# Wide operands for keys and values in a two-layer hybrid decoder step on one Trainium2 core

## What is computed

```
h = rmsnorm(x, g_attn)
(q_a, kv_cmp, kv_slc, kv_win, gate_a, q_b, k_b, v_b, r_b, lr_b, merge) = split(h @ w_in)
kv_slc, kv_win = qk_norm_rows(kv_slc, g_k_slc), qk_norm_rows(kv_win, g_k_win)
o_cmp = cmp_attend(q, compress_kv(past + kv_cmp)); o_slc = top-16 blocks; o_win = window of 512
o_a = sigmoid(gate_a) weighted sum of o_cmp, o_slc, o_win
log_a = log_sigmoid(lr_b @ w_gate_up + b_gate) / 16
o_b, S_new = gla_scan(q_b, k_b, v_b, log_a, state_gla)
x = x + (sigmoid(g_ma) * (o_a @ w_pa) + sigmoid(g_mb) * (o_b @ w_pb)) @ w_out
x = x + (gelu(conv3(h2 @ w_u)) * (h2 @ w_g)) @ w_down,  h2 = rmsnorm(x, g_ffn)
```

## Time and profile before

| | |
|---|---|
| median of three runs | 2159.13 us (2158.03 to 2160.08) |
| the profiled execution, its own time | 2148.94 us |
| its span | 2147.2 us, 30516 instructions |
| PE, matmuls | 2107.1 us, 98% of the span, 11911 records |
| DVE, ACT, POOL | 1144.9, 516.2, 675.8 us (53%, 24%, 31%) |
| mean granted TensorE clock | 0.994 of full speed |
| one weight slot | 512.0 KB, 4.8 us from issue to landing (w_in) |

### The profile page before, as it was taken

How to read it: one execution, slowest core, us unless ns; L and a number is a source line. 1 busy time by engine, 2 the same in 40 slices (tenths; PEclk the granted TensorE clock), 3 DMA queues, 4 the chain that set the end, 5 groups by cost and what they waited for, 6 DMA issues and landing times.

```text
span 2147.2 us, 30516 instructions
## 1 busy us (share of the span) xinstructions
PE 2107.1 (98%) x11911; PEld 1687.4 (79%) x11911; DVE 1144.9 (53%) x2384; ACT 516.2 (24%) x1108; POOL 675.8 (31%) x789
## 2 busy tenths in 40 slices
PE   8999989999999999999999999999999999999999
PEld 7787866678888888888887877666788888888887
DVE  5566746755337455453336666567453454555522
ACT  3124124532112222210122232244221222222000
POOL 5240042204223444434331400621232234444332
PEclk9999999999999999999999999999999999999999
DMA  5874631113222222222284736201132222222222
GB/s 155 273 236 181 248 118 40 41 43 101 79 82 79 79 79 89 90 79 74 68 291 120 267 136 273 81 28 32 59 104 82 79 79 79 79 89 91 79 69 75
DMA packets 172305, 237.53 MB, mean 111 GB/s; under 512 B 39551, under 2 KB 151680, under 8 KB 169408
## 3 DMA queue, kind: packets, MB, share of 16 engines
q1 hardware_dynamic: 153320, 133.11, 20.6%
q0 software_dynamic: 18400, 102.36, 12.8%
q10 hardware_dynamic: 444, 0.12, 0.0%
HBM read 222.76 MB, written 21.11 MB: 114 GB/s over the span
## 4 chain that ended last, share of the span: by engine, by line
PE 91%; DVE 2%; ACT 2%; POOL 2%; DMA 2%; issue 1%; SPq 0%; POOLq 0%; DVEq 0%; ACTq 0%
PE PS L1005 52%; PE PS L948 10%; PE PS L1163 6%; PE PS L970 5%; PE PS L996 3%; PE PS L1499 2%; PE PS L1416 2%; PE PS L460 2%; PE PS L1427 2%; DMA arena<-in_cache_kv_slc_dram,idx 2%; ACT arena L1710 1%; POOL arena L835 1%; PE PS L1374 1%; PE PS L1399 1%; PE PS L1548 1%
## 5 line engine op out<-in xcount | busy, mean ns | idle before, releaser
L1005 PE MATMUL PS<-arena,ring 128*128 128x272 f32 x1632 | 401.3, 393 | 0.9 <-DVE xT L2076 0.6
L1005 PEld LDWEIGHTS PS<-arena,ring 128*128 128x128 f32 x1632 | 309.3, 190 | 65.9 <-issue 2.4
L1710 ACT ACTIVATE arena<-PS 128x272 f32<-128x272 f32 (+12 forms) x442 | 176.1, 423 | 739.6 <-PE PS L1005 286.4
L2076 DVE TENSOR_TENSOR arena<-PS,arena 128x272 f32<-128x272 f32 (+4 forms) x298 | 138.7, 476 | 370.8 <-PE PS L1005 279.4
L1005 PE MATMUL PS<-hT,ring 128*128 128x272 f32 x1120 | 282.3, 397 | 5.9 <-DVE arena L2076 4.7
L1005 PEld LDWEIGHTS PS<-hT,ring 128*128 128x128 f32 x1120 | 213.6, 192 | 52.8 <-DVE arena L2076 5.2
L2076 DVE TENSOR_TENSOR xT<-PS,xT 128x272 f32<-128x272 f32 x224 | 99.0, 442 | 252.2 <-PE PS L1005 251.9
L862 POOL TENSOR_TENSOR qT<-ring 128x512 f32<-128x512 f32 (+1 forms) x38 | 48.8, 1284 | 384.7 <-PE PS L1005 255.7
L2082 DVE SCALAR_TENSOR_TENSOR arena<-arena,prm 128x32 f32<-128x32 f32 (+1 forms) x176 | 143.8, 817 | 22.1 <-ACT arena L1710 18.2
L948 PE MATMUL PS<-hT,ring 128*128 128x272 f32 x640 | 150.7, 394 | 2.3 <-DVE small L2373 1.5
L1005 PE MATMUL PS<-arena,kv_kT 128*128 128x272 f32 x616 | 149.7, 392 | 0.0
(11 more groups left out here) (362 smaller groups left out, 2989.7 us busy)
## 6 DMA issues: line engine op xcount, KB each, us to landing
ring<-in_w_up_dram SPq DMA_DIRECT2D x88, 512.0 KB, 4.6
ring<-in_w_in_dram SPq DMA_DIRECT2D x68, 512.0 KB, 4.8
ring<-in_w_down_dram SPq DMA_DIRECT2D x32, 512.0 KB, 4.4
arena<-in_state_kv_win_dram POOLq DMA_DIRECT2D x4, 2048.0 KB, 8.3
ring<-in_w_out_dram SPq DMA_DIRECT2D x16, 512.0 KB, 4.3
out_dram<-in_state_kv_win_dram POOLq DMA_DIRECT2D x2, 4064.0 KB, 39.6
ring<-in_w_down_dram SPq DMA_DIRECT2D x16, 384.0 KB, 3.5
ring<-in_w_in_dram SPq DMA_DIRECT2D x16, 256.0 KB, 4.6
```

Of the source, the lines that this page charges most:

```text
L1005: mm = pe.matmul(PS[:, bank, 0:HALF], weight[:, k, :], rhs(k), start=(start and k == 0), stop=(stop and k == kc - 1), skip_group_check=not ...
L1710: return nc.scalar.activation(out, in_, func, **kw)
L2076: return nc.vector.tensor_tensor(out, a, b_, op)
```

## The change

Four edits, the same in both layers.

1. `kv1` and `kv2` are multiplied together: a view over two ring slots gives moving operands of 2 x 256 = 512 columns (`wide_few` for the sampled rows, `wide_tiles` for the token tiles). The tickets are `kv12b`, `kv12l` (tiles 0 and 1) and `kv12h` (tiles 2 and 3); ACT copies each out in two parts.
2. The linear branch's values are done the same way from `vb0` and `vb1`, one tile per ticket (`vb0` to `vb3`, and `vbf3` for the sampled rows), at earlier places; `qb` and `kb` come behind them, and the ring's order is changed to fit. The second half of `kb` is split over two places by token halves (`kb1l`, `kb1h`).
3. POOL issues the `S0` loads behind its sums of `hT` and of `rb1`.
4. ACT does one more unit of exponentials ahead of each decay step.

```diff
-    steps = ["q0", "q1", "kv1", "kv2", "kv0", "gl", "qb", "kb", "vb0", "vb1", "rb0", "rb1"]
+    steps = ["q0", "q1", "kv1", "kv2", "kv0", "gl", "vb0", "vb1", "qb", "kb", "rb0", "rb1"]
...
-    at = {("s", 0, 5): ("vb00",), ("s", 0, 4): ("vb01",), ("s", 0, 3): ("qb0",), ("s", 0, 2): ("qb1",), ("s", 0, 1): ("kb0",), ("s", 0, 0): ("kb1",),
-          ("b", 0): ("vb0b", "vb0h"), ("b", 1): ("vb1l",), ("b", 2): ("vb1h", "vb1b"), ("s", 1, 0): ("rb00",), ("u", 0): ("rb01",)}
+    at = {("s", 0, 5): ("vb0",), ("s", 0, 4): ("vb1",), ("s", 0, 3): ("vb2",), ("s", 0, 2): ("vbf3", "vb3"), ("s", 0, 1): ("qb0",),
+          ("s", 0, 0): ("qb1",), ("b", 0): ("kb0",), ("b", 1): ("kb1l",), ("b", 2): ("kb1h",), ("s", 1, 0): ("rb00",), ("u", 0): ("rb01",)}
...
-                for b in range(NB):
-                    gp.dma_start(S0[:, b, :, :], ins["state_gla"][one, b].rearrange("o (a c) k v -> (o c k) a v", c=2)).then_inc(*S.inc(gp, "s0_in", 16))
...
                 in_pieces(low[:, :, HALF:NT], high[:, :, HALF:NT], low[:, :, HALF:NT], ALU.subtract, HALF // 2)
                 gp.nop().then_inc(*S.inc(gp, "g_sum"))
+                gp.nop().then_inc(*S.inc(gp, "settled"))
+                for b in range(NB):
+                    gp.dma_start(S0[:, b, :, :], ins["state_gla"][one, b].rearrange("o (a c) k v -> (o c k) a v", c=2)).then_inc(*S.inc(gp, "s0_in", 16))
...
+            def wide_weights(names):
+
+                for name in names:
+                    pe.wait_ge(*w_landed(pe, name))
+                s0, s1 = sorted(wslot(name)[0] for name in names)
+                return ring[:, s0:s1 + 1:s1 - s0, :].rearrange("p j (k n) -> p j k n", n=WCOLS)
...
+            def wide_tiles(ticket, names, tiles, pool="T"):
+
+                w = wide_weights(names)
+                pe.wait_ge(*S.claim(pe, pool, ticket))
+                b = S.banks(pe, ticket)
+                for j, t in enumerate(tiles):
+                    for k in range(KC):
+                        mm = pe.matmul(PS[:, b + j, :].rearrange("p (j n) -> p j n", j=2), hT[:, k, P * t:P * t + P], w[:, :, k, :], start=(k == 0), stop=(k == KC - 1))
...
-                s = wload("kv1")
-                few("kv1b", s, 256)
-                tm("kv1a", s, 0, 256, 256, range(4))
+                wide_few("kv12b", ("kv1", "kv2"))
+                wide_tiles("kv12l", ("kv1", "kv2"), (0, 1))
...
+                wide_tiles("kv12h", ("kv1", "kv2"), (2, 3))
...
+                def wide_key(ticket, t):
+
+                    act.wait_ge(*S.filled(act, ticket))
+                    b = S.banks(act, ticket)
+                    run(kv[:, t:t + 2, 2, :], PS[:, b:b + 2, 0:256], ACT.Copy)
+                    run(kv[:, t:t + 2, 1, :], PS[:, b:b + 2, 256:512], ACT.Copy).then_inc(*S.drain(act, ticket))
...
+                    if j in DECAY_EXP_AT:
+                        exps(done)
+                        done += 1
                     decay_step(DECAY_EXP_AT.get(j))
...
-                for j in (1, 2):
-                    dv.wait_ge(*S.drained(dv, f"kv{j}a"))
+                for j in "lh":
+                    dv.wait_ge(*S.drained(dv, f"kv12{j}"))
```

More of the change, by code:

```diff
@@ L241, in last_ticket @@
     if name[0] in "qkvr" and name[:2] != "kv":
-        return {"q0": "q1", "q1": "q3", "vb0": "vb0h", "vb1": "vb1b"}.get(name, name + "1")
+        return {"q0": "q1", "q1": "q3", "vb0": "vb3", "vb1": "vb3", "kb": "kb1h"}.get(name, name + "1")
     if name[:2] == "kv":
-        return name + "a"
+        return "kv0a" if name == "kv0" else "kv12h"
     if name[:2] in ("pa", "pb"):
@@ L616, in _ @@
                             (dst[:, :, 24:40], w_in[one, :, O_LR:O_LR + 16].rearrange("o (k p) n -> p (o k) n", p=P))])
-                for name, c0 in (("qb", O_QB), ("kb", O_KB), ("vb0", O_VB), ("vb1", O_VB + 256), ("rb0", O_RB), ("rb1", O_RB + 256)):
+                for name, c0 in (("vb0", O_VB), ("vb1", O_VB + 256), ("qb", O_QB), ("kb", O_KB), ("rb0", O_RB), ("rb1", O_RB + 256)):
                     cols_of(name, w_in, c0)
@@ L980, in few, with wide_few @@
                     mm = pe.matmul(PS[q:q + NS, b, 0:n], hT[:, k, SEQ:NT], w[:, k, :], start=(k < 4), stop=(k >= 4))
+                mm.then_inc(*S.fill(pe, ticket))
+            def wide_weights(names):
[3 more added lines that the diff above has]
+                return ring[:, s0:s1 + 1:s1 - s0, :].rearrange("p j (k n) -> p j k n", n=WCOLS)
+            def wide_few(ticket, names):
+                w = wide_weights(names)
+                pe.wait_ge(*S.claim(pe, "T", ticket))
+                b = S.banks(pe, ticket)
+                for k in range(KC):
+                    q = NS * (k % 4)
+                    mm = pe.matmul(PS[q:q + NS, b, :].rearrange("p (j n) -> p j n", j=2), hT[:, k, SEQ:NT], w[:, :, k, :], start=(k < 4), stop=(k >= 4))
+                mm.then_inc(*S.fill(pe, ticket))
+            def wide_tiles(ticket, names, tiles, pool="T"):
+                w = wide_weights(names)
+                pe.wait_ge(*S.claim(pe, pool, ticket))
+                b = S.banks(pe, ticket)
+                for j, t in enumerate(tiles):
+                    for k in range(KC):
+                        mm = pe.matmul(PS[:, b + j, :].rearrange("p (j n) -> p j n", j=2), hT[:, k, P * t:P * t + P], w[:, :, k, :], start=(k == 0), stop=(k == KC - 1))
                 mm.then_inc(*S.fill(pe, ticket))
@@ L1327, in small_values @@
                     b = S.banks(pe, "vbf")
-                    for name in ("vb0b", "vb1b"):
-                        pe.wait_ge(*S.drained(pe, name))
+                    pe.wait_ge(*S.drained(pe, "vbf3"))
                     pe.matmul(PS[0:NS, b, :], fold4[:, :], vbs, start=True, stop=True).then_inc(*S.fill(pe, "vbf"))
@@ L1766, in _ @@
                     query(r)
-                value_key(1)
+                act.wait_ge(*S.filled(act, "kv12b"))
+                b = S.banks(act, "kv12b")
+                run(kvs[:, 2, :], PS[:, b, 0:256], ACT.Copy)
+                run(kvs[:, 1, :], PS[:, b, 256:512], ACT.Copy).then_inc(*S.drain(act, "kv12b"))
+                wide_key("kv12l", 0)
                 for r in range(R):
                     query_root(r)
-                value_key(2)
+                wide_key("kv12h", 2)
                 act.wait_ge(*S.filled(act, "kvf"))
@@ L2321, in side_copy @@
                             dv.wait_ge(*S.at(dv, "x_stored"))
-                            cc = slice(256 * int(name[2]), 256 * int(name[2]) + 256)
-                            if name[3] == "b":
-                                move = copy(vbs[:, cc], PS[:, b, 0:256])
-                            else:
-                                t0, t1 = {"0": (0, 1), "1": (1, 2), "l": (0, 2), "h": (2, 4)}[name[3]]
-                                move = copy(vT[:, t0:t1, cc], PS[:, b, 0:256 * (t1 - t0)].rearrange("p (t n) -> p t n", n=256))
+                            move = copy(vbs if name == "vbf3" else vT[:, int(name[2]), :], PS[:, b, :])
+                        elif name[-1] in "lh":
+                            a = "lh".index(name[-1])
+                            move = copy(kbT[:, int(name[2]), HALF * a:HALF * a + HALF], PS[:, b, 0:HALF])
                         else:
@@ L2643, in decay_step @@
                     if step == "q":
-                        for name in ("qb0", "qb1", "kb0", "kb1"):
+                        for name in ("qb0", "qb1", "kb0", "kb1l", "kb1h"):
                             dv.wait_ge(*S.drained(dv, name))
```

39 lines of the change are left out of this document (21 added, 18 removed).

## The result

| | before | after |
|---|---|---|
| median | 2159.39 us (2158.03 to 2160.08, 4 runs) | 2183.55 us (2181.72 to 2185.88, 4 runs) |
| the profiled execution | 2148.94 us | 2185.88 us |
| mean granted TensorE clock in it | 0.994 | 0.984 |

The changed kernel is slower by 24.2 us, a ratio of 1.0113 with a 95% interval of 1.0096 to 1.0131. The forecast was 2176.8 in a range of 2164 to 2188, slower with 0.88: the sign was right, the size short by 6.7 us.

A forecast was written before the change was run, and what follows sets the result against it. TensorE was taken as the bound, 91% of layer 0's chain of waits. Terms summed to +8.35 us in layer 0 and +9.35 in layer 1, together +17.7, giving a median of 2176.8 in a range of 2164 to 2188.

The forecast's parts named there:

- Linear values moved forward: Compression loop and behind it: two wide side products on the chain, +3.4 us each; third place loses records, -0.65.
- The two buffer waits: Before the first block scores: PE waits 3.4 us for T0, 5.8 for T1, until DVE drains them; +10.6 per layer.
- Rival B: Before the first block scores: DVE drains T0 and T1 in time, so no waits; 2148 us; chance 0.07.
- The slow clock behind them: At the two new waits before block scores: slow restarts of 1.7 us each, +3.4 per layer, between 0 and 5.
- Rival A: At the new waits: clock not lowered, 3.4 and 1.5 us fall away per layer; +7.9, 2167; chance 0.16.
- Gather stretch: Gathers to second block scores: -1.6 and -0.4 us, slow restart +1.5; together -0.5, between -2.7 and +1.
- State loads and exponentials: Units: PE's waits for POOL and DVE and their restarts go; -6.5 and -5.5 us by layer, -4.2 in each.
- Rival C: Units: gains not had, another wait stands behind the one removed; up to +20 us, half of it 2187; chance 0.10.
- Keys and values: Keys and values, each layer: 64 records of 512 columns replace 128 of 256; -0.6 us, between -1.2 and 0.
- the figure that the prediction had set aside: Keys and values: the Trainium skill's 2.5 ns per record removed, 0.16 us saved, against 0.3 to 0.6 by the rows.
- From profile to median: Whole kernel: median 2159.13 is 10.2 us above the profiled 2148.94; the same difference kept for the forecast, 2176.8.
- Two of the signs: New profile: first block scores 26 to 31 us behind the end of oc, second 25 to 28 behind the gathers' start.

The follow-up runs named there:

- e7: The changed kernel with vb3 ahead of vbf3 and DVE's two copies ahead of the block distances and two transposes; 2154.11 us, ratio to before 0.9976.
- e4: The kernel before with only the linear values wide and moved forward, with the ring order and kb split that go with them; 2198.87 us, ratio 1.0184.
- e8: The changed kernel with both buffer waits kept but filled with extra PE products; 2177.41 us, 6.1 less than the changed kernel.
- e1: The kernel before with only the state loads moved behind POOL's sums; 2146.82 us, ratio 0.9937.
- e2: The kernel before with only one more unit of exponentials ahead of each decay step; 2154.57 us, ratio 0.9974.
- e3: The kernel before with only the keys and values kv1 and kv2 multiplied together; 2159.29 us, ratio 1.0002.
- second profile of before: The kernel before, unchanged, profiled a second time; 2155.30 us in one execution, against 2148.94 in its first profile.

## Why the prediction was right, and where it was short

- **Linear values moved forward** (+3.4 +3.4 -0.65): +6.83 over the stretch with the first two, -0.46 for the third. Right.
- **The two buffer waits** (3.4 and 5.8): 3.74 and 5.82, in both layers, ended by the DVE instructions that were named. Rival B asked for drains by 1.9 and 14 us; they did not come. e7 shows that the waits and their restarts were the whole of it: with other buffers the place costs 1.4 us, and the kernel is 5.2 faster than before, where B had 2148.
- **The slow clock behind them** (1.7 each, 0 to 5 for both) is the term that was mis-sized. It cost 2.9 and 3.0 in either layer (9.98 and 10.05 for 7.13; 10.56 and 10.59 for 7.60), so 2.4 to 2.5 more per layer, 4.9 in all, and above the prediction's own bound of 5 for both in one layer. The first wait was 0.3 longer than forecast too. The step that failed is taking one price from rows of another work: the rows at the units gave 1.6 to 2.6, and the same wait of 3.74 was followed by anything from nothing (e4) to 2.9. Rival A (no clock cost) is out: e8 takes the cost away by keeping PE busy.
- **Gather stretch** (-0.5, within -2.7 and +1): -0.7 and +0.3. The gathers to the scores took 2.5 less (2.0 was worked out) and the slow scores cost 1.8 (1.5).
- **State loads and exponentials** (-10.7 and -9.7 together): -10.3 and -9.1 in the units. Rival C is out there, since e1 has its whole gain alone. What the prediction had at nothing is the stretch behind the units: its clock can fall while PE is busy (e2), and it is 1.3 and 0.6 longer than in the first profile of before, 1.3 and 1.6 longer than in the second.
- **Keys and values** (-0.6): -0.78 in layer 1 and no more than the noise in medians (e3). In layer 0 the stall hides it. The split was wrong, though. The prediction read 0.220 us per record out of 14.08/64, which has the first record's start-up in it; behind that the records start 0.216 apart at 256 columns and 0.429 at 512. By these steps the multiplication itself gains 0.16 per layer, the figure that the prediction had set aside, and the other 0.6 lie around it.
- **From profile to median.** "I put the same difference on the median" took the 10.2 us as a constant, without a cause for it. That it nearly held is in part luck: the stall is missing from the first profile of before and stands in the 13 others, those of the changed kernel and of the second run of before among them, so it falls out of the difference of medians. That it is most of the 10.2 is likely and not shown, since the second profile, which has it, is still 5.1 us under its median. Of the 12.8 us by which the profiles lie further apart than the medians, 10.5 are the first profile's distance under its median and 2.3 the other's above its own.
- **Two of the signs** lie outside what was named: the first block scores came 32.8 us behind the end of `oc` (26 to 31), by the restarts, and the second ones 24.7 behind the gathers (25 to 28).

Against the second profile of before the changed one is 30.6 us longer, 12.9 over the forecast of 17.7. Of that, 5.6 is the place before the first block scores (4.9 the restarts, 0.7 the longer first wait), 3.0 the stretch behind the units, and 2.8 the way to the keys of layer 1, where the stall is; the rest lies in differences of about 1 us or less. In the medians 6.5 are left over. That the same clock terms make them up is likely, since the place before the scores alone has 5.6, but no run shows it for the medians.

## What to carry to other kernels

Before a piece of work is put in front of a wait, list which buffer each claim will take in turn and who drains it, in that engine's own serial order: here one more ticket turned two free buffers into two waits, and swapping two tickets and two copies gave back 29 us. Price an idle TensorE at its wait plus a restart between nothing and 3 us, not at one number. And take a second profile before a stretch is costed from one: here a profile 10 us under its median lacked a stall that the 13 others had.

## What was not expected of the hardware

- The same wait of 3.74 us was followed by nothing, 1.6, 2.9 and 2.9 us of extra time for the same 16 records (7.11, 8.71, 9.98, 10.05, against 7.13 with no wait).
- The granted clock fell to 0.50 in a stretch in which PE was busy all the time, 2.8 to 4.7 us after the start of 64 records of 32x128, in 12 of 28 passes through the same code, at a cost of 1.1 to 2.8 us. Which passes is told by where the stretch lies against the moments at which the clock changes, and not by the edit.
- Beside gathers that hold the DMA share at 1.04, PE and ACT stop together for up to 6 us, with "issue", each other or an unknown queue as reasons, in 13 of 14 profiles, and the clock falls to 0.50 behind most of the stops; moving the gathers moved the stops at about the same cost.
